# Attention C's scores on halves and strips of the TensorE array, and three loads and waits in another order

## The chip, the cores and the metric

One core of one Trainium2 chip runs the whole program in one launch. The metric is device microseconds (us) of that core, from the first to the last instruction with what the launch adds. TensorE (PE) multiplies, VectorE (DVE), ScalarE (ACT) and GpSimd (POOL) do the rest, and DMAs are issued from the queues of SyncE (SP) and ScalarE.

## The reference

A sequence of 1024 tokens of width 1024 passes a first block (four recurrent branches, a feed-forward part) and two attention layers. Two places matter here.

```python
# first block, feed-forward part (D_FF = 2816)
gate_up = xn @ w_ffn_in
g_ff, u_ff = jnp.split(gate_up, [D_FF], axis=-1)
h = h + (jax.nn.silu(g_ff) * u_ff) @ w_ffn_out
# second attention layer, attention C: 8 heads of 64 + 32 dimensions
q  = (rmsnorm(cq, g_cq) @ w_cq_b).reshape(B, S, 8, 96)
kv = (rmsnorm(ckv, g_ckv) @ w_ckv_b).reshape(B, S, 8, 64 + 64)
qc = rmsnorm(q, gq_c)                                      # then its last 32 rotated
kc = rmsnorm(concat([k_nope, k_pe of all heads], -1), gk_c) # then its last 32 rotated
oc = attend_blocks(qc, kc, v_c, 96 ** -0.5)                # softmax(q k^T) v
```

## The kernel before

Activations lie transposed: a tile `A(i)` (all of them in `AR`) or `R(i)` (in `ARR`) holds 128 features by 1024 tokens. PSUM is four tiles `ps` of 128 by 1024. TensorE's results go round these four: the n-th job (`opn`) takes tile n modulo 4 and first waits until the job four before it has been read (`freed`). So the order in which jobs are opened decides who waits for whom. Weights come in tiles `WR` (four of them), loaded by SyncE's queue in the order of the list `loads`, each when the job four weights earlier is done. Where fp32 is split into a high and a low part, GpSimd does it in the order of the list `splits`: a cast `WH<-WR` and a subtraction `WL<-WR,WH` (in the pairs also `ARR<-AR`).

**Feed-forward part.** Hidden tiles 0, 1 and 21 are plain products. The other 38 products go in 19 pairs by block products: seven half-size products (`product`, twelve matmuls each) in place of eight. They need sums of the weights (`weight_sums`, four VectorE subtractions or additions on 128x512) and sums of the input (`t_sum`, sixteen of 128x512 into `A(0..7)`), which ScalarE rounds to a high part (`R(16+j)`) and VectorE turns into a low part (`R(j)`, eight subtractions on 128x1024, semaphore `s_tlow`). The pairs' weights alternate between `A(8..11)` (even pairs) and `WR` (odd pairs); in the even case `A(8)` and `A(9)` receive the raw weights, so the first two of the four rounds of `t_sum` must have read them. GpSimd splits a pair's weights in four slots (`s_pair_split`), the first three of 128x1024, the last of 128x512. Then `ffn_out` multiplies the hidden tiles in three groups of 8, 8 and 6. A group's tiles are read back from HBM (`hidden` in `loads`), rounded by ScalarE (`hid_hi`) and subtracted by VectorE (`hid_lo`).

**Attention C.** `attend_pairs` makes 32 steps, eight blocks of 128 queries for each of four pairs of heads. In step s TensorE makes the scores `S` of both heads of block s (line 1273 of before), the output `O` of block s-2 (line 1284), and the transposes `T` of the probabilities of block s-1 (line 1295); `weave` then appends a piece of side work. On VectorE a step takes the maximum of each head's scores (line 3306), and ScalarE makes the exponentials (line 2375), whose end frees the score's PSUM tile, and then copies the transposes out (line 2385). Jobs per step are S0, S1, O, T0, T1. So T1 waits for the first exponential, and whatever TensorE opens behind T1 waits for the second:

```python
mm = pe.matmul(pt[:, h * 512:h * 512 + 512], q(p, m)[0:96, rows],
               k(p, m)[0:96, h * 512:h * 512 + 512], start=True, stop=True)
```

Attention B has the same steps, with head dimension 64: head 0 on rows 0 to 63 of the array and head 1 on rows 64 to 127, in turns. Beside C's steps the next heads are prepared, `prep_c(h)` in four steps a head, h from 2 to 7, and `prep_d(0)` in eight. For a head, TensorE makes query and key (lines 348), VectorE rotates the query's last 32 rows with three 32x1024 operations (`rotate`), and ScalarE scales and squares the key's own 64 rows and copies and squares the 32 rows that all heads share. Heads 4 and 6 also have a gate product (48 matmuls) in the step of the key. `prep_c0` prepares heads 0 and 1 ahead of the steps.

## Time and profile before

| | us |
|---|---|
| median of 3 runs | 3873.71 (3873.5 to 3878.88) |
| the profiled execution | 3871.55 |
| its span, first to last instruction | 3869.5 |
| mean granted TensorE clock | 0.984 |

The profile gives for each engine its busy time and its idle time with what ended it. A timeline row merges equal instructions in a row; a matmul on fp32 operands shows as two records, so the four score matmuls of a step are eight records.

### The profile page before, as it was taken

The page shows a single profiled execution, that of the slowest core. Times are in us where ns is not written, and L with a number is a line of the kernel's source. Part 1 is how long each engine was busy: PE and PEld are TensorE (multiplying, and loading weights), DVE is VectorE, ACT ScalarE, POOL GpSimd, SP SyncE. Part 2 cuts the span into 40 slices and gives each one's busy share as a digit, 9 for nine tenths or more (in the row PEclk, how much of TensorE's full clock was granted, in tenths as well). Part 3 has the DMA queues.
Part 4 walks back from the last instruction along what each step waited for, and adds up shares of the span by engine and source line. Part 5 has one row for each costly group of instructions (what it writes and reads, how often), then busy time and mean ns, then how long its engine had stood idle before and what let it go on. Part 6 is the DMA issues. An engine that isn't in the chain of part 4 may idle for free.

```text
span 3869.5 us, 51841 instructions
## 1 busy us (share of the span) xinstructions
PE 3706.4 (96%) x21561; PEld 2909.6 (75%) x21561; DVE 1985.1 (51%) x2505; ACT 1325.9 (34%) x1603; POOL 1018.0 (26%) x634
## 2 busy tenths in 40 slices
PE   8999999999999999999899999999999999999988
PEld 6778888878788887888788777666677566667767
DVE  8464455524652526333412556665754655456673
ACT  3243333322330112111201344455623666444450
POOL 4212222222233335666433411110022001111011
PEclk9999999999999999999999999999999999999999
DMA  4111111111125422222522211100121001111011
GB/s 146 34 50 50 44 53 47 50 44 47 55 79 182 147 88 66 86 83 82 195 78 70 85 43 43 44 17 9 53 66 54 14 13 27 31 25 25 17 55 68
DMA packets 283160, 238.56 MB, mean 62 GB/s; under 512 B 16976, under 2 KB 255728, under 8 KB 282928
## 3 DMA queue, kind: packets, MB, share of 16 engines
q1 hardware_dynamic: 262128, 166.04, 14.6%
q10 hardware_dynamic: 20800, 69.22, 5.0%
q8 instruction: 172, 2.82, 0.3%
q14 instruction: 60, 0.49, 0.0%
HBM read 181.81 MB, written 49.35 MB: 60 GB/s over the span
## 4 chain that ended last, share of the span: by engine, by line
PE 82%; DVE 11%; ACT 4%; issue 3%; POOL 1%; ACTq 0%; DMA 0%; DVEq 0%; SPq 0%; POOLq 0%
PE ps L401 19%; PE ps L418 18%; PE ps L451 15%; PE ps L902 9%; DVE AR L2474 3%; PE ps L1273 2%; DVE AR L2482 2%; DVE SM L3306 2%; PE ps L701 2%; PE ps L1284 1%; PE ps L1264 1%; PE ps L1295 1%; PE ps L503 1%; PE ps L1344 1%; PE ps L348 1%
## 5 line engine op out<-in xcount | busy, mean ns | idle before, releaser
L3439 POOL CAST WH<-WR 128x1024 fp32r<-128x1024 f32 (+2 forms) x231 | 240.8, 1043 | 2587.4 <-DMA WR<-in_w_in 827.1
L3441 POOL TENSOR_TENSOR WL<-WR,WH 128x1024 fp32r<-128x1024 f32 (+2 forms) x231 | 502.8, 2177 | 18.5
L2474 DVE TENSOR_TENSOR AR<-AR 128x512 f32<-128x512 f32 (+3 forms) x426 | 454.1, 1066 | 56.5 <-ACT AR L1822 38.1
L418 PE MATMUL ps<-ARR,WH 128*128 128x512 f32 x1472 | 367.1, 391 | 12.9 <-issue 10.7
L418 PEld LDWEIGHTS ps<-ARR,WH 128*128 128x128 f32 x1472 | 277.4, 189 | 71.6 <-issue 11.1
L401 PE MATMUL ps<-XH,WH 128*128 128x512 f32 (+2 forms) x1168 | 299.2, 399 | 4.6 <-POOL WL L3441 2.2
L401 PE MATMUL ps<-XH,WL 128*128 128x512 f32 (+2 forms) x1168 | 289.8, 390 | 0.0
L401 PE MATMUL ps<-XL,WH 128*128 128x512 f32 (+2 forms) x1168 | 288.6, 389 | 0.0
L401 PEld LDWEIGHTS ps<-XH,WH 128*128 128x128 f32 (+2 forms) x1168 | 215.9, 188 | 57.8 <-issue 8.0
L3306 DVE TENSOR_REDUCE SM<-ps 128x1 f32<-128x1024 f32 x128 | 156.8, 1225 | 197.3 <-PE ps L1273 116.1
L401 PEld LDWEIGHTS ps<-XH,WL 128*128 128x128 f32 (+2 forms) x1168 | 218.0, 187 | 48.8
L2474 DVE TENSOR_TENSOR H<-H,ps 128x1024 f32<-128x1024 f32 (+1 forms) x68 | 78.8, 1159 | 341.0 <-PE ps L418 340.7
L401 PEld LDWEIGHTS ps<-XL,WH 128*128 128x128 f32 (+2 forms) x1168 | 217.0, 186 | 48.0
L451 PE MATMUL ps<-XH,WH 128*128 128x512 f32 x864 | 236.5, 418 | 3.7 <-ACT AR L2315 2.3
L2482 DVE SCALAR_TENSOR_TENSOR AR<-ps,AR 128x512 f32<-128x512 f32 (+2 forms) x122 | 59.3, 486 | 341.5 <-ACT AR L1574 227.7
L2474 DVE TENSOR_TENSOR AR<-ps,AR 128x128 f32<-128x128 f32 (+2 forms) x193 | 102.1, 529 | 254.2 <-PE ps L902 220.7
L451 PE MATMUL ps<-XH,WL 128*128 128x512 f32 x864 | 214.4, 390 | 0.0
L451 PE MATMUL ps<-XL,WH 128*128 128x512 f32 x864 | 213.4, 389 | 0.0
L451 PEld LDWEIGHTS ps<-XH,WH 128*128 128x128 f32 x864 | 161.1, 197 | 57.3 <-issue 19.9
L451 PEld LDWEIGHTS ps<-XH,WL 128*128 128x128 f32 x864 | 163.1, 189 | 35.1
L451 PEld LDWEIGHTS ps<-XL,WH 128*128 128x128 f32 x864 | 162.2, 188 | 33.7
L2375 ACT ACTIVATE AR<-ps,SM,AR 128x1024 f32<-128x1024 f32 x112 | 135.0, 1205 | 152.2 <-DVE SM L2482 145.9
(295 smaller groups left out, 6257.3 us busy)
## 6 DMA issues: line engine op xcount, KB each, us to landing
WR<-in_w_in SPq DMA_DIRECT2D x78, 512.0 KB, 3.8
gates<-AR ACTq DMA_DIRECT2D x54, 512.0 KB, 2.8
AR<-gates SPq DMA_DIRECT2D x54, 512.0 KB, 4.3
H<-spill ACTq DMA_DIRECT2D x32, 512.0 KB, 5.9
WR<-in_w_in_e SPq DMA_DIRECT2D x26, 512.0 KB, 3.8
spill<-H ACTq DMA_DIRECT2D x24, 512.0 KB, 2.7
WR<-in_w_ffn_in SPq DMA_DIRECT2D x24, 512.0 KB, 3.8
WR<-in_w_in_o SPq DMA_DIRECT2D x23, 512.0 KB, 3.9
```

What stands on the lines that cost most here:

```text
L401: mm = pe.matmul(pt[0:m, h * 512:h * 512 + 512], wp[:, slot, k, 0:m], xp[:, k, h * 512:h * 512 + 512], start=i == 0, stop=i == 3 * KD - 1)
L418: mm = pe.matmul(pt[:, h * 512:h * 512 + 512], wp[:, w % 4, k, :], xp(k)[:, h * 512:h * 512 + 512], start=i == 0, stop=i == 3 * nk - 1)
L451: mm = pe.matmul(pt[:, h * 512:h * 512 + 512], wp[:, w % 4, k, :], xp[:, k, h * 512:h * 512 + 512], start=i == 0, stop=i == 3 * KD - 1)
L701: mm = pe.matmul(out, x1[r, c], later, start=True, stop=True)
L902: mm = pe.matmul(out, wp(i, slot)[:, 4 * half + k, :], xp(k), start=first and n == 0, stop=n == 11, skip_group_check=True)
L1273: mm = pe.matmul(pt[:, h * 512:h * 512 + 512], q(p, m)[0:96, rows], k(p, m)[0:96, h * 512:h * 512 + 512], start=True, stop=True)
L2375: act.activation(PROB[kind][i], PS[bank(("S", b, m))][:, :], ACT.Exp, scale=row_scale(kind, s, m), bias=SM[:, 20 + i:21 + i], accum_out=SM ...
L2474: return v.tensor_tensor(o, x, y, op)
L2482: return v.scalar_tensor_tensor(out=o, in0=x, scalar=s, in1=y, op0=op0, op1=op1)
L3306: v.tensor_reduce(SM[:, 34 + m:35 + m], PS[bank(("S", b, m))][:, :], AX.X, ALU.max)\
L3439: pool.tensor_copy(hi, full).then_inc(s_whi, 1)
L3441: pool.tensor_tensor(lo, full, hi, ALU.subtract).then_inc(s_wsplit, 1)
```

## The change

**Scores.** Each head's 96 rows are contracted in two parts. First 64 rows: head 0 on rows 0 to 63 of the array, head 1 on rows 64 to 127, as in attention B. Then the other 32 rows, as a strip of 32: the four matmuls (two heads, two halves of the keys) stand on four different strips. For that the even head has its 32 rotated rows twice, at rows 64 and 96, and the odd head has its own 64 at rows 64 to 127 and the rotated rows at 0 and 32. So the odd head's weights load in three parts, `rotate` has a fourth operation (`again`), and ScalarE copies the shared key rows twice.

**Block products.** VectorE makes the first pair's `weight_sums(0)` ahead of the eight low parts, and those in the order 0 to 7; TensorE's second product waits for four low parts, the third for eight; SyncE loads the first pair's weights after eight input sums.

**`ffn_out`.** The first two weights stand ahead of the hidden tiles' loads in SyncE's queue.

```diff
@@ block products and the list of loads (TensorE) @@
-                    pe.wait_ge(s_tlow, KD)
+                    pe.wait_ge(s_tlow, 4)
                 product(xz[:, 512:L], i, 1, 0, t_hi(0), t_lo(0)).then_inc(s_products, 1)
                 pe.wait_ge(freed[ny % 4], ny // 4)
+                if i == 0:
+                    pe.wait_ge(s_tlow, KD)
                 product(wy[:, 0:512], i, 1, 1, t_hi(3), t_lo(3)).then_inc(s_products, 1)
...
-            loads.append(("hidden", 0))
-            loads.append(("hidden", 1))
...
-                    if g == 1 and f == 4:
-                        loads.append(("hidden", 2))
+                    if (g, f) in ((0, 1), (0, 3), (1, 4)):
+                        loads.append(("hidden", {1: 0, 3: 1, 4: 2}[f]))
@@ prep_c, prep_c0 (TensorE) @@
+            def query_c(h):
+                if h % 2:
+                    gemm(("qc", h), (cols(wcq, h * 96 + 64, 32, nk=2), cols(wcq, h * 96, 64, nk=2)),
+                         rhs=lambda k: A(18 + k), nk=2)
+                else:
+                    gemm(("qc", h), cols(wcq, h * 96, 96, nk=2), rhs=lambda k: A(18 + k), m=96, nk=2)
+            def key_c(h):
+                gemm(("kc", h), cols(wckv, h * 128, 64, nk=1), rhs=lambda k: A(28), m=64, nk=1, at=h % 2 * 64)
@@ attend_pairs, kind "C" (TensorE) @@
-                            for m in range(2):
-                                pt, n = opn(("S", b, m))
+                            two = [opn(("S", b, m)) for m in range(2)]
+                            for pt, n in two:
                                 pe.wait_ge(freed[n % 4], n // 4)
...
+                            for h in range(2):
+                                for m, (pt, n) in enumerate(two):
+                                    e = slice(m * 64, m * 64 + 64)
+                                    pe.matmul(pt[:, h * 512:h * 512 + 512], q(p, m)[e, rows],
+                                              k(p, m)[e, h * 512:h * 512 + 512], start=True, stop=False,
+                                              skip_group_check=True)
+                            for h in range(2):
+                                for m, (pt, n) in enumerate(two):
+                                    e = slice(64 - m * 64 + h * 32, 96 - m * 64 + h * 32)
+                                    mm = pe.matmul(pt[:, h * 512:h * 512 + 512], q(p, m)[e, rows],
+                                                   k(p, m)[e, h * 512:h * 512 + 512], start=False, stop=True,
+                                                   skip_group_check=True)
+                                    if h:
+                                        mm.then_inc(filled[n % 4], 1)
@@ load (SyncE) @@
+                if isinstance(src, tuple) and m == P:
+                    for c in (0, 32):
+                        sp.dma_start(dst[:, 0:nk, c:c + 32], src[0]).then_inc(s_half_in, 16)
+                    sp.wait_ge(s_half_in, 16 * (dups[0] + 2))
+                    dups[0] += 2
+                    src, dst = src[1], dst[:, 0:nk, 64:P]
...
-                            sp.wait_ge(s_tsum, 16)
+                            sp.wait_ge(s_tsum, 8)
@@ prep_c (ScalarE), c = shared_at(h) @@
-                act.activation(kt[64:96, :], A(9)[96:128, :], ACT.Copy).then_inc(s_act_step, 1)
-                act.wait_ge(s_act_step, tick(s_act_step))
-                act.activation(A(22)[64:96, :], A(8)[96:128, :], ACT.Square).then_inc(s_kraw, 1)
+                for g in (c, c + 32):
+                    act.activation(kt[g:g + 32, :], A(26)[96:128, :], ACT.Copy).then_inc(s_act_step, 1)
+                    act.wait_ge(s_act_step, tick(s_act_step))
+                act.activation(A(22)[c:c + 32, :], A(25)[96:128, :], ACT.Square).then_inc(s_kraw, 1)
@@ block products, rotate (VectorE) @@
-            for n, j in enumerate((0, 4, 1, 5, 2, 6, 3, 7)):
-                v.wait_ge(s_thigh, n + 1)
+            weight_sums(0)
+            for j in range(KD):
+                v.wait_ge(s_thigh, 2 * (j % 4) + 1 + j // 4)
                 TT(R(j), A(j), R(16 + j), ALU.subtract).then_inc(s_tlow, 1)
                 v.wait_ge(s_tlow, tick(s_tlow))
-            weight_sums(0)
...
+                if again is not None:
+                    TT(x[again, :], x[rows, :], tmp[rows, :], ALU.add).then_inc(s_dve_step, 1)
+                    v.wait_ge(s_dve_step, tick(s_dve_step))
                 TT(x[rows, :], x[rows, :], tmp[rows, :], ALU.add).then_inc(s_rope_tmp, 1)
```

The instructions of the engines stand in another order at three places. SyncE's queue between the feed-forward part's last pair and `ffn_out`, before (`gates` holds the hidden tiles):

```order
117 L1511 DMA AR<-in_w_ffn_in 128x8x128
118 L1455 DMA WR<-in_w_ffn_in 128x8x128 x2
119 L1523 DMA AR<-gates 128x1024 x16
120 L1455 DMA WR<-in_w_ffn_out 128x8x128 x13
121 L1523 DMA AR<-gates 128x1024 x6
122 L1455 DMA WR<-in_w_ffn_out 128x8x128 x3
```

The same place of the changed program:

```order
117 L1538 DMA AR<-in_w_ffn_in 128x8x128
118 L1482 DMA WR<-in_w_ffn_in 128x8x128 x2
119 L1482 DMA WR<-in_w_ffn_out 128x8x128 x2
120 L1550 DMA AR<-gates 128x1024 x8
121 L1482 DMA WR<-in_w_ffn_out 128x8x128 x2
122 L1550 DMA AR<-gates 128x1024 x8
123 L1482 DMA WR<-in_w_ffn_out 128x8x128 x9
124 L1550 DMA AR<-gates 128x1024 x6
125 L1482 DMA WR<-in_w_ffn_out 128x8x128 x3
```

Two `ffn_out` weights now stand ahead of the first eight hidden tiles, and two more ahead of the next eight.

VectorE at the start of the block products, before, from the fifth of the eight low parts on (`ARR0`, `ARR1` are the low parts, `AR<-AR 128x512 x4` the weight sums of the first pair):

```order
468 L2474 TENSOR_TENSOR ARR0_51<-AR,ARR4_55 128x1024
469 L2474 TENSOR_TENSOR ARR1_52<-AR,ARR5_56 128x1024
470 L2474 TENSOR_TENSOR ARR0_51<-AR,ARR4_55 128x1024
471 L2474 TENSOR_TENSOR ARR1_52<-AR,ARR5_56 128x1024
472 L2474 TENSOR_TENSOR AR<-AR 128x512 x4
473 L2474 TENSOR_TENSOR AR<-AR,ps3 128x1024
474 L2474 TENSOR_TENSOR WR<-WR 128x512 x4
```

The changed program, from the input sums on:

```order
462 L2519 TENSOR_TENSOR AR<-AR 128x512 x16
463 L2519 TENSOR_TENSOR AR<-AR,ps1 128x1024
464 L2519 TENSOR_TENSOR AR<-AR 128x512 x4
465 L2519 TENSOR_TENSOR ARR0_51<-AR,ARR4_55 128x1024 x4
466 L2519 TENSOR_TENSOR ARR1_52<-AR,ARR5_56 128x1024 x4
467 L2519 TENSOR_TENSOR AR<-AR,ps3 128x1024
468 L2519 TENSOR_TENSOR WR<-WR 128x512 x4
```

The weight sums moved from behind the eight low parts to ahead of them.

TensorE in a step of attention C with a query's product behind it (line 348, in the changed program 349), before (scores on line 1273, in the changed program halves on 1286 and strips on 1292):

```order
2350 L1273 MATMUL ps<-AR 128x512 x4
2351 L1284 MATMUL ps<-AR 64x128 x16
2352 L1295 MATMUL ps<-CST,AR 128x128 x8
2353 L1295 MATMUL ps<-CST,MSK 128x128 x8
2354 L348 MATMUL ps<-AR,WR 96x512 x4
```

The same step of the changed program:

```order
2359 L1286 MATMUL ps<-AR 128x512 x4
2360 L1292 MATMUL ps<-AR 128x512 x4
2361 L1305 MATMUL ps<-AR 64x128 x16
2362 L1316 MATMUL ps<-CST,AR 128x128 x8
2363 L1316 MATMUL ps<-CST,MSK 128x128 x8
2364 L349 MATMUL ps<-AR,WR 96x512 x4
```

Four score matmuls became four on halves and four on strips; what follows them is the same.

## Rows read from the trace of the kernel before

**Rows 1.** The page's busy time of each engine: busy us, share of the span, instructions.
```profile
PE 3706.4 (96%) x21561; PEld 2909.6 (75%) x21561; DVE 1985.1 (51%) x2505; ACT 1325.9 (34%) x1603; POOL 1018.0 (26%) x634
```

**Rows 2.** Timeline, SyncE's DMA queue alone: start us, us, engine line, out<-in, count.
```profile
1856.67 0.99 SPq L1455 DMA_DIRECT2D WR<-in_w_ffn_in  x2
```

**Rows 3.** Timeline 1868 to 1912, start of `ffn_out`; in brackets: idle before, releaser.
```profile
1875.71 12.09 SPq L1523 DMA_DIRECT2D AR<-gates  x16
...
1887.85 22.12 SPq L1455 DMA_DIRECT2D WR<-in_w_ffn_out  x4
...
1891.58 1.06 ACT L1940 ACTIVATE ARR<-AR 128x1024 fp32r<-128x1024 f32 x1 [0.21 <-DMA AR<-gates]
...
1904.85 3.20 POOL L3441 TENSOR_TENSOR WL<-WR,WH 128x1024 fp32r<-128x1024 f32 x1
...
1908.15 3.72 PE L418 MATMUL ps<-ARR,WH 128*128 128x512 f32 x8 [10.71 <-issue]
```

**Rows 4.** Timeline, the next matmuls of `ffn_out`.
```profile
1911.70 2.02 PE L418 MATMUL ps<-ARR,WL 128*128 128x512 f32 x8
```

**Rows 5.** Busy us (instructions) of PE, PEld, DVE, ACT, POOL; PEclk, DMA share, GB/s.
```profile
1902.00:1911.00 9.00, 2.85 (x7) 2.30 (x8) 6.47 (x4) 7.51 (x8) 4.24 (x2) 0.50 1.07 382
```

**Rows 6.** Timeline 1462 to 1496, VectorE beside GpSimd, then the first pair's weights.
```profile
1469.61 10.53 DVE L2474 TENSOR_TENSOR XL<-AR,XH 128x1024 fp32r<-128x1024 f32 x4
...
1471.83 1.92 POOL L3439 CAST WH<-WR 128x1024 fp32r<-128x1024 f32 x1
...
1477.14 1.92 POOL L3439 CAST WH<-WR 128x1024 fp32r<-128x1024 f32 x1
...
1488.12 2.16 ACT L1947 ACTIVATE ARR<-AR 128x1024 fp32r<-128x1024 f32 x2 [0.71 <-DVE AR L2474]
...
1493.87 0.37 SPq L1508 DMA_DIRECT2D AR<-in_w_ffn_in  x1
```

**Rows 7.** Timeline 1490 to 1545, the first block products.
```profile
1495.13 10.04 DVE L2474 TENSOR_TENSOR ARR<-AR,ARR 128x1024 fp32r<-128x1024 f32 x8
...
1505.21 2.87 DVE L2474 TENSOR_TENSOR AR<-AR 128x512 f32<-128x512 f32 x4
...
1511.72 3.78 PE L902 MATMUL ps<-XH,ARR 128*128 128x512 f32 x8 [6.71 <-POOL ARR L3451]
...
1530.08 2.88 PE L902 MATMUL ps<-ARR,ARR 128*128 128x512 f32 x12
...
1532.80 1.07 PE L902 MATMUL ps<-XH,WH 128*128 128x512 f32 x4
```

**Rows 8.** Timeline 2593 to 2607, one step of attention B with nothing beside it.
```profile
2593.15 1.99 PE L1264 MATMUL ps<-AR 64*128 64x512 f32 x8 [0.30 <-ACT AR L2375]
...
2595.24 1.23 DVE L3306 TENSOR_REDUCE SM<-ps 128x1 f32<-128x1024 f32 x1 [1.09 <-PE ps L1264]
...
2596.69 1.23 DVE L3306 TENSOR_REDUCE SM<-ps 128x1 f32<-128x1024 f32 x1
...
2599.58 1.99 PE L1264 MATMUL ps<-AR 64*128 64x512 f32 x8 [0.30 <-ACT AR L2375]
```

**Rows 9.** Timeline 3111 to 3167, two steps of attention C.
```profile
3111.31 3.60 PE L1273 MATMUL ps<-AR 96*128 96x512 f32 x8
...
3115.01 1.22 DVE L3306 TENSOR_REDUCE SM<-ps 128x1 f32<-128x1024 f32 x1 [0.30 <-PE ps L1273]
...
3118.54 1.84 PE L984 MATMUL ps<-CST,AR 96*128 96x2 f32 x16
...
3138.38 1.05 ACT L2231 ACTIVATE AR<-AR 32x1024 f32<-32x1024 f32 x1
...
3139.47 1.21 ACT L2375 ACTIVATE AR<-ps,SM,AR 128x1024 f32<-128x1024 f32 x1
```

**Rows 10.** Timeline 3082 to 3120, VectorE rotates a query of attention C.
```profile
3081.24 3.72 DVE L2474 TENSOR_TENSOR AR<-AR 32x1024 f32<-32x1024 f32 x3
```

**Rows 11.** Chain of work that ended last, before attention C: start us, us, what.
```profile
3002.39 1.23 DVE AR L2474
```

More of the change, by code:

```diff
@@ L54 @@
 CE = CEPS2 + 1
-CW = {n: CE + 8 + i * 70 for i, n in enumerate(["w64", "w96", "w128", "w256", "w1024", "weps"])}
+CW = {n: CE + 8 + i * 70 for i, n in enumerate(["w64", "w96", "w128", "w256", "w1024", "weps", "w96_odd"])}
 NCST = CE + 8 + len(CW) * 70
@@ L347, in gemm @@
                     for k in range(nk):
-                        mm = pe.matmul(pt[0:m, h * 512:h * 512 + 512], WR[0:kp, w % 4, k, 0:m],
+                        mm = pe.matmul(pt[at:at + m, h * 512:h * 512 + 512], WR[0:kp, w % 4, k, 0:m],
                                        rhs(k)[0:kp, h * 512:h * 512 + 512], start=k == 0, stop=k == nk - 1)
@@ L1268, in attend_pairs @@
                         else:
-                            for m in range(2):
-                                pt, n = opn(("S", b, m))
+                            two = [opn(("S", b, m)) for m in range(2)]
+                            for pt, n in two:
                                 pe.wait_ge(freed[n % 4], n // 4)
-                                for h in range(2):
-                                    mm = pe.matmul(pt[:, h * 512:h * 512 + 512], q(p, m)[0:96, rows],
-                                                   k(p, m)[0:96, h * 512:h * 512 + 512], start=True, stop=True)
-                                mm.then_inc(filled[n % 4], 1)
+                            for h in range(2):
[12 more added lines that the diff above has]
+                                        mm.then_inc(filled[n % 4], 1)
                     if s >= 2:
@@ L2092, in tables @@
             def tables(which):
-                act.dma_start(A(25), a["rope"][2 * which]).then_inc(s_tab_in, 16)
-                act.dma_start(A(26), a["rope"][2 * which + 1]).then_inc(s_tab_in, 16)
+                rows = slice(0, 96 if which == 1 else P)
+                act.dma_start(A(25)[rows, :], a["rope"][2 * which][rows, :]).then_inc(s_tab_in, 16)
+                act.dma_start(A(26)[rows, :], a["rope"][2 * which + 1][rows, :]).then_inc(s_tab_in, 16)
             def gate(name, dst):
@@ L2194, in shared_key, with shared_at, own_rows, own_gain @@
             def shared_key(h, square):
-                act.activation(A(CK[h % 4])[64:96, :], A(9)[96:128, :], ACT.Copy).then_inc(s_act_step, 1)
-                act.wait_ge(s_act_step, tick(s_act_step))
-                act.activation(square[64:96, :], A(8)[96:128, :], ACT.Square).then_inc(s_act_step, 1)
-                act.wait_ge(s_act_step, tick(s_act_step))
+                for r in (0, 32):
+                    act.activation(A(CK[h % 4])[shared_at(h) + r:shared_at(h) + r + 32, :], A(26)[96:128, :], ACT.Copy)\
+                        .then_inc(s_act_step, 1)
+                    act.wait_ge(s_act_step, tick(s_act_step))
+                act.activation(square[shared_at(h):shared_at(h) + 32, :], A(25)[96:128, :], ACT.Square)\
+                    .then_inc(s_act_step, 1)
+                act.wait_ge(s_act_step, tick(s_act_step))
+            def shared_at(h):
+                return 0 if h % 2 else 64
+            def own_rows(h):
+                return slice(h % 2 * 64, h % 2 * 64 + 64)
+            def own_gain(h):
+                c = PC["gkc_odd" if h % 2 else "gkc"]
+                return PAR[own_rows(h), c:c + 1]
             def own_key(h, square):
                 act.wait_ge(filled[bank(("kc", h))], turn(("kc", h)))
-                t = PS[bank(("kc", h))]
-                act.activation(A(CK[h % 4])[0:64, :], t[0:64, :], ACT.Copy, scale=par("gkc", 0, 64)).then_inc(s_act_step, 1)
+                t, r = PS[bank(("kc", h))], own_rows(h)
+                act.activation(A(CK[h % 4])[r, :], t[r, :], ACT.Copy, scale=own_gain(h)).then_inc(s_act_step, 1)
                 act.wait_ge(s_act_step, tick(s_act_step))
-                act.activation(square[0:64, :], t[0:64, :], ACT.Square)\
+                act.activation(square[r, :], t[r, :], ACT.Square)\
                     .then_inc(freed[bank(("kc", h))], 1)
@@ L2213, in prep_c @@
                 act.wait_ge(s_rope_tmp, 6 + h)
-                raw(("qc", h), A(CQ[h % 4]), A(22), 96, par("gqc", 0, 96), (A(27), (64,), 16, s_rot_in[0]))
+                if h % 2:
+                    raw(("qc", h), A(CQ[h % 4]), A(22), P, par("gqc_odd"), (A(27), (0,), 16, s_rot_in[0]))
+                else:
+                    raw(("qc", h), A(CQ[h % 4]), A(22), 96, par("gqc", 0, 96), (A(27), (64,), 16, s_rot_in[0]))
                 yield
@@ L3068, in _, with rotate @@
             turns = [0, 0]
-            def rotate(x, tmp, ndma, rows=slice(0, P), i=0):
+            def rotate(x, tmp, ndma, rows=slice(0, P), i=0, again=None):
                 turns[i] += 16 * ndma
@@ L3120, in prep_c0 @@
                 for h in range(2):
[L3121 removed]
+                    kb(A(CK[h]), P, ("hb", cnt["hn"] - 2 + h))
                 yield
@@ L3126, in prep_c @@
                 hq(RS[h % 4], 96 ** -0.5)
-                rotate(A(CQ[h % 4]), A(27), 2, slice(64, 96))
+                rotate(A(CQ[h % 4]), A(27), 2, *((slice(0, 32), 0, slice(32, 64)) if h % 2 else (slice(64, 96), 0, slice(96, P))))
                 yield
@@ L3130, in prep_c @@
                 yield
-                kb(A(CK[h % 4]), 96)
+                kb(A(CK[h % 4]))
                 yield
@@ L3481, in constants @@
         cst[:min(n, P), CW[f"w{n}"] + 6:CW[f"w{n}"] + 8] = 1.0 / n
+    for r in (slice(0, 32), slice(64, P)):
+        cst[r, CW["w96_odd"] + 6:CW["w96_odd"] + 8] = 1.0 / 96
     cst[:, CW["weps"] + 6:CW["weps"] + 8] = EPS / 1024
@@ L3520, in constants @@
     table(0, "pB", [(b + o, 16, ang) for b in (0, 64) for o, ang in ((0, row), (32, col))])
-    table(1, "pC", [(64, 16, angles(t, 32, 10000.0))])
+    table(1, "pC", [(b, 16, angles(t, 32, 10000.0)) for b in (0, 64)])
     part = angles(t, 16, 500000.0)
@@ L3563, in pack @@
     put("gkc", g("gk_c_2")[0])
+    for k, n in (("gqc_odd", "gq_c_2"), ("gkc_odd", "gk_c_2")):
+        put(k, np.concatenate([g(n)[0][64:], g(n)[0][64:], g(n)[0][:64]]))
     put("gsub", g("g_sub_d_2")[0])
```

42 lines of the change are left out of this document (21 added, 21 removed).

## The prediction

> **What bounds the kernel now.** I read the page first: TensorE is busy for 96% of the span [rows 1], so what counts is its idle time and its own work. Then the chain of waits, for its longest single waits, and the timeline at those places. Two are in the feed-forward part: 10.71 us ahead of `ffn_out` [rows 3] and 6.71 us ahead of the first block product [rows 7]. Then the timeline of attention C, step by step, to see what ends each wait there; a step counts here from its first score matmul to the first side job behind T1. Fifteen of C's 32 steps have a light one: the score matmuls start at 3111.31, VectorE's second maximum at 3115.01 (3.70 later), and TensorE reaches the job behind T1 at 3118.54, after 7.23 [rows 9]; fourteen of them take 7.15 to 7.31, the fifteenth is the last step, below. Nothing waits in them: they are TensorE's own work. Attention B shows the same step with scores on halves. There the first maximum starts 2.09 after the scores (2593.15 to 2595.24), and the next scores start 4.34 after that maximum, held by the second exponential, not by TensorE [rows 8].
>
> **The `ffn_out` weights.** Before, SyncE issued sixteen hidden tiles from 1875.71 to 1887.80 and only then the weight, whose low part GpSimd ended at 1904.85 + 3.20 = 1908.05; TensorE started at 1908.15, 10.71 late [rows 3]. Changed, two weights stand right behind the last `ffn_in` weights, issued from 1856.67 [rows 2], some 31 us earlier. What is late next are the hidden tiles: group 0's last high part ended at 1891.58 + 1.06 = 1892.64 [rows 3], 4.8 us before TensorE's place at 1908.15 - 10.71 = 1897.44. So the wait goes whole. The wait also cost clock: in 1902 to 1911 the granted clock was 0.50 [rows 5], that is 1.2 and not 2.4 GHz, and the first eight matmuls took 1911.70 - 1908.15 = 3.55 [rows 3, 4] where twelve take 1532.80 - 1530.08 = 2.72 [rows 7], so eight 1.81: 1.74 more. Term: -(10.71 + 1.74) = **-12.4**. The second group's tiles move back behind two more weights; they are wanted eight jobs later, and cost nothing. If that cover were gone, at most the old 10.7 would come back.
>
> **The first block products.** Wanted is a start at 1511.72 - 6.71 = 1505.01. Half the input sums are done at 1488.12, so the weights can be issued 1493.87 - 1488.12 = 5.75 earlier [rows 6], and are there when VectorE gets to the weight sums at 1495.13 (its place for the low parts before). These take 2.87, to 1498.0; before they ran from 1505.21 [rows 7]. GpSimd's first slot is then in time for 1505. But now GpSimd splits while VectorE makes the eight low parts, of the same kind (128x1024 to fp32r, two SBUF inputs) as four that ran beside GpSimd's splits a little earlier: those took 10.53, that is 2.63 each, and GpSimd needed 1477.14 - 1471.83 = 5.31 for a slot [rows 6]; alone, eight low parts took 10.04, 1.26 each [rows 7]. So the second slot and the fourth low part are both ready at about 1498.0 + 10.6 = 1508.6, when the first product (2.72) has ended at 1507.7: 0.9 lost. The third product wants all eight. GpSimd's three full slots take 15.9 and cover six low parts; for the last two beside the short slot I estimate half a slot and one op alone, 2.65 + 1.26 = 3.9: 1498.0 + 15.9 + 3.9 = 1517.8. TensorE stands again from 1511.3, 6.5 us, and pays the clock again: before, the seven products took 1532.80 - 1511.72 = 21.08 where 7 x 2.72 = 19.04 are due, 2.04 more. End of the first pair: 1517.8 + 5 x 2.72 + 2.04 = 1533.4, against 1532.80 [rows 7]: **+0.6**. If the two engines do not hinder each other, all is in time and -(6.71 + 2.04) = -8.8 results; that is the lower bound. Upper: both fully one after the other, 8 x 2.63 = 21 to 1519, +1.8.
>
> **The scores.** From B to C the second set of four rounds on the array puts the maximum from 2.09 to 3.70 after the start [rows 8, 9]. Changed, there are four matmul slots on halves (as B's) and one round in which four strips run together, half as long as B's whole: six units for B's four and C's eight, so (2.09 + 3.70) / 2 = 2.90. No row shows four strips at once, nor a change from halves to strips. Upper bound: strips run only two at a time, eight units, 3.70. I take 3.05, close to the lower, since two halves ran fully together in B. TensorE saves 0.65 us a step by that, some 21 us over 32 steps, and that is not what the kernel gets: both heads' scores now end together, so the first maximum starts at 3.05 and no longer while the second head's scores are still made, and the job behind T1 comes 4.34 after it [rows 8], at 7.39. Against 7.23 [rows 9] a light step is 0.16 *longer*: fourteen make +2.2 (bounds 7.24, +0.1; 8.04, +11). In the last step TensorE waits for copies behind the second exponential; the second maximum moves from 3.70 to 3.05 + 1.45 (2596.69 - 2595.24 [rows 8]) = 4.50: +0.8. In the five steps with the key's norm in front, the first maximum stands behind VectorE's work on that norm, before and after: nothing. The first two steps, the one behind the first key and the three of `prep_d(0)` with longer chains I take at nothing, between -1 and +1 together.
>
> The Trainium skill ("TensorE: Matmul & The Clock Gate", Part 3) gives four row strips a measured 3.07 times the speed of one after another, not four times; by it the strip round would be 0.26 longer if 0.80 is its length at four times. The skill ("TensorEngine Tiling (Array Packing)", Key Properties) also says that changing the tiling mode drains TensorE, which speaks against two modes in a step. By both, a light step comes to about 7.5, and the fourteen to +4 instead of +2.2.
>
> **The preparation of heads.** Of six heads, four (2, 3, 5, 7) have the rotation on VectorE directly ahead of the step's first maximum: three operations in 3.72 [rows 10], 1.24 each. The fourth adds **1.24** to the step. For heads 4 and 6 the gate product covers the rotation, but ScalarE's work on the key runs to the exponential: copies and squares end 3138.38 + 1.05 = 3139.43, the first exponential starts at 3139.47 [rows 9]. One more copy adds **1.05**. Scores ending earlier help neither. Sum 4 x 1.24 + 2 x 1.05 = +7.1. In `prep_c0` both rotations are on the chain that ended last, six pieces of 1.23 from 3002.39 on [rows 11]; two more make +2.5. ScalarE's extra copies there lie beside the second gate product. The odd queries' weights load in three parts with a wait between; they are issued about a head, four steps, ahead, and even the load behind sixteen others took only 1887.85 to about 1903.7 [rows 3]. Uncovered, it would cost a landing, some 5 us, in four heads.
>
> **Sum** against the profiled execution's 3871.55 us (span 3869.5 and 2.05 around it; the median, 3873.71, is 2.2 above): -12.4 + 0.6 + 2.2 + 0.8 + 7.1 + 2.5 = +0.8. Some clock will be lost at the longer waits of the key's steps, for one of which I add 0.5 on average: 3872.9, and on the scale of the median **3875.0**. A difference under 0.2%, 7.7 us, can't be told from none.
>
> **Rivals.**
> - *No hindrance at the block products.* VectorE and GpSimd overlap freely: -8.8 in place of +0.6, 3866. Against it stand rows 6. Chance 0.10, half of it on the faster side.
> - *The key's steps have slack.* If the added operations find room there (the steps' waits are inferred from releasers), +7.1 falls away: 3868. Chance 0.08.
> - *The scores gain what TensorE saves.* 0.65 x 32 = -21 in place of +2.2 and +0.8: 3851. It needs the exponentials earlier than 4.34 behind the first maximum, and B, in the same code, shows they aren't. Chance 0.05.
> - *Strips run two at a time* (or the change of mode costs as much): maximum at 3.70, light steps 8.04; fourteen of them and the five behind the norm 0.81 each, the last 3.70 + 1.45 - 3.70 = 1.45: 16.8 in place of 3.0, 3889, slower. It decides from 3.4 on. Chance 0.12.
> - *The clock falls in the key's steps.* They wait at T1 for the exponential already, and now 1.05 to 1.24 longer. If each of six loses what `ffn_out`'s start lost (1.74), +10.4: 3885, slower; four of six are enough. Chance 0.15.
> - The forecast, 3869 to 3881: 0.50.
>
> **Numbers.** Range 3865 to 3887: it leaves out the scores' full gain, most of the two-at-a-time case, and little else. Faster by over 0.2% (under 3866): 0.05, half of 0.10, and 0.03 of the second rival: 0.13. Slower (over 3881.4): 0.12 + 0.15 and 0.01: 0.28. Within: 0.59.
>
> **What the changed profile would show.** TensorE goes into `ffn_out` with no wait over 1 us and no half clock. At the block products the first starts near 1505, and one wait of 5 to 7 us stands ahead of the third, ended by VectorE; low parts of 2 to 3 us beside GpSimd. In C the halves and strips end about 3.0 after their start, the first maximum 3.05, the job behind T1 7.4, its wait ended by the exponential (line 2375 before); key steps 1.05 to 1.24 longer. I am wrong if light steps get shorter than 7.1, or if the low parts take 1.26 each beside the splits.

## The result and the profile after

The changed kernel takes 3895.28 us (median of 5 runs, 3893.64 to 3903.11), the kernel before 3873.71 beside it: 1.0055 of it, 95% interval 1.0041 to 1.0069. It is slower by 21.6 us, where I had said 1.3, and outside my range. The profiled execution took 3894.96, its span 3893.0, with a mean granted clock of 0.982.

**Into `ffn_out`** the wait is gone. The timeline there; the first row is GpSimd's subtraction for the second `ffn_out` weight, its last one before a gap of 18 us:

```profile
1872.94 2.41 POOL L3489 TENSOR_TENSOR WL<-WR,WH 128x1024 fp32r<-128x1024 f32 x1
...
1897.36 1.98 PE L419 MATMUL ps<-ARR,WH 128*128 128x512 f32 x8
```

Both weights are split at 1872.94 + 2.41 = 1875.35, and TensorE starts at 1897.36 straight behind its own work (no idle time stands in the row). Before it was 1908.15 [rows 3].

**The first block products**, again the timeline:

```profile
1497.74 18.64 DVE L2519 TENSOR_TENSOR ARR<-AR,ARR 128x1024 fp32r<-128x1024 f32 x8
...
1504.56 1.98 PE L903 MATMUL ps<-XH,ARR 128*128 128x512 f32 x8
...
1508.54 3.01 PE L903 MATMUL ps<-ARR,ARR 128*128 128x512 f32 x12 [1.10 <-POOL ARR L3499]
...
1516.52 8.37 PE L903 MATMUL ps<-ARR,ARR 128*128 128x512 f32 x24 [4.97 <-DVE ARR L2519]
...
1532.88 1.07 PE L903 MATMUL ps<-XH,WH 128*128 128x512 f32 x4
```

Eight low parts take 18.64, 2.33 each; the first product starts at 1504.56, TensorE waits 1.10 ahead of the second and 4.97 ahead of the third, and the pair ends at 1532.88, where it ended at 1532.80 [rows 7]. That is the picture forecast, place by place.

**Attention C** is where the time went. From its first score matmul to attention D's first transposes, 408.3 us before (3017.19 to 3425.52) became 444.4 (3005.45 to 3449.86): +36.1, where I had some 10 in these steps. A light step (nothing in front of the maxima but the scores) without a split of a weight, step 16, steps counted from 0:

```profile
3192.04 1.99 PE L1286 MATMUL ps<-AR 64*128 64x512 f32 x8 [1.53 <-issue]
...
3193.96 1.14 PE L1292 MATMUL ps<-AR 32*128 32x512 f32 x8
...
3195.03 1.97 PE L1305 MATMUL ps<-AR 128*64 128x128 f32 x32
3195.22 1.22 DVE L3354 TENSOR_REDUCE SM<-ps 128x1 f32<-128x1024 f32 x1 [3.38 <-PE ps L1292]
3196.48 0.16 DVE L2527 SCALAR_TENSOR_TENSOR SM<-SM,AR 128x1 f32<-128x1 f32 x1
...
3197.93 0.16 DVE L2527 SCALAR_TENSOR_TENSOR SM<-SM,AR 128x1 f32<-128x1 f32 x1
...
3198.20 1.06 PE L1316 MATMUL ps<-CST,MSK 128*128 128x128 f32 x8 [0.17 <-ACT AR L2420]
3198.21 1.21 ACT L2420 ACTIVATE AR<-ps,SM,AR 128x1024 f32<-128x1024 f32 x1 [0.16 <-DVE SM L2527]
...
3199.56 3.67 PE L349 MATMUL ps<-AR,WR 128*96 128x512 f32 x8 [0.30 <-ACT AR L2420]
```

Halves from 3192.04, strips from 3193.96, the scores' end at 3195.03, after 2.99. The first maximum starts 3.18 after the scores, the job behind T1 (3199.56) 4.34 after that, 7.52 in all: the forecast had 3.05, 4.34 and 7.39. TensorE now waits in such a step, 0.17 and 0.30, where it did not wait at all. A step in which GpSimd splits a weight (step 12) looks otherwise:

```profile
3146.53 1.99 PE L1286 MATMUL ps<-AR 64*128 64x512 f32 x8
...
3149.71 1.23 DVE L3354 TENSOR_REDUCE SM<-ps 128x1 f32<-128x1024 f32 x1 [3.69 <-PE ps L1292]
3150.65 1.04 POOL L3487 CAST WH<-WR 128x1024 fp32r<-128x1024 f32 x1 [98.89 <-DMA WR<-in_w_in_o]
3150.97 0.73 DVE L2527 SCALAR_TENSOR_TENSOR SM<-SM,AR 128x1 f32<-128x1 f32 x1
...
3151.76 2.36 POOL L3489 TENSOR_TENSOR WL<-WR,WH 128x1024 fp32r<-128x1024 f32 x1
...
3152.99 1.15 DVE L2527 SCALAR_TENSOR_TENSOR SM<-SM,AR 128x1 f32<-128x1 f32 x1
...
3154.25 1.20 ACT L2420 ACTIVATE AR<-ps,SM,AR 128x1024 f32<-128x1024 f32 x1 [1.15 <-DVE SM L2527]
...
3155.69 1.06 PE L469 MATMUL ps<-CST,AR 128*128 128x128 f32 x8 [1.37 <-ACT AR L2420]
```

The small operation behind a maximum (128x1, two operands: it negates and scales it for the exponential) takes 0.73 in place of 0.16, and the second 1.15. Both end just behind GpSimd's instruction: 3150.97 + 0.73 = 3151.70 and GpSimd's cast 3150.65 + 1.04 = 3151.69; 3152.99 + 1.15 = 3154.14 and the subtraction 3151.76 + 2.36 = 3154.12. The second exponential starts at 3154.25, 7.72 after the scores, and the job behind T1 at 9.16, not 7.52. The same step of the kernel before:

```profile
3153.60 3.60 PE L1273 MATMUL ps<-AR 96*128 96x512 f32 x8
...
3156.85 0.16 DVE L2482 SCALAR_TENSOR_TENSOR SM<-SM,AR 128x1 f32<-128x1 f32 x1
...
3157.77 1.04 POOL L3439 CAST WH<-WR 128x1024 fp32r<-128x1024 f32 x1 [90.99 <-DMA WR<-in_w_in_o]
...
3158.56 0.26 DVE L2482 SCALAR_TENSOR_TENSOR SM<-SM,AR 128x1 f32<-128x1 f32 x1
3158.89 2.37 POOL L3441 TENSOR_TENSOR WL<-WR,WH 128x1024 fp32r<-128x1024 f32 x1
3158.94 1.21 ACT L2375 ACTIVATE AR<-ps,SM,AR 128x1024 f32<-128x1024 f32 x1 [0.52 <-DVE SM L2482]
...
3159.72 2.08 DVE L2478 TENSOR_SCALAR AR<-AR,SM 128x1024 f32<-128x1024 f32 x1
```

GpSimd's split began 4.17 after the scores' start, where it is 4.12 now, but the small operations stood at 3.25 and 4.96: one ahead of it, the other at the end of the cast (0.26, to 3158.82; the cast ends at 3158.81). The large operation at 3159.72 did wait, 2.08, and nobody waited for it.

**A step with the key's norm in front** (step 15) has a wait on VectorE that I had ruled out. Ahead of its first maximum VectorE now stands idle 0.48 for the last strips, where before the maximum followed VectorE's own work on the norm without such a wait (at 2.76 after the scores' start; now 3.18):

```profile
3184.92 1.23 DVE L3354 TENSOR_REDUCE SM<-ps 128x1 f32<-128x1024 f32 x1 [0.48 <-PE ps L1292]
```

T1's waits for the exponential in C (TensorE, 3000 to 3450: line waited at, total, times, longest), and C's window, whose granted clock (third number from the end) is 0.95 of full speed:

```profile
PE ps L1316 <- ACT AR L2420: 19.5, 30, 2.9
```

```profile
3005.00:3450.00 445.00, 396.28 (x2870) 259.68 (x2871) 238.98 (x393) 230.76 (x293) 33.90 (x20) 0.95 0.08 19
```

Before, T1's line had 5.8 us of such waits in 5 places, and in C the clock was 0.99. By the trace's record of the clock, 41.0 us of C now ran at half clock, and 10.7 before:

```profile
PE ps L1295 <- ACT AR L2375: 5.8, 5, 1.4
```

```profile
3017.00:3425.00 408.00, 390.34 (x2610) 264.40 (x2611) 226.02 (x386) 224.43 (x287) 34.01 (x20) 0.99 0.09 21
```

### The profile page after: what moved, and what is told of

It is laid out like the page before. It is cut to its first block, busy times and chain, and to the rows that moved or that the text cites. A ratio compares the mean times of both kernels' runs of the same rounds, so it can differ in the third digit from the quotient of the medians.

```text
span 3893.0 us, 52410 instructions
## 1 busy us (share of the span) xinstructions
PE 3707.5 (95%) x21817; PEld 2903.6 (75%) x21817; DVE 1998.5 (51%) x2513; ACT 1334.5 (34%) x1611; POOL 1021.3 (26%) x634
## 3 DMA queue, kind: packets, MB, share of 16 engines
q8 instruction: 174, 2.85, 0.3%
## 4 chain that ended last, share of the span: by engine, by line
PE 79%; DVE 13%; ACT 4%; issue 3%; POOL 0%; DMA 0%; ACTq 0%; SPq 0%; DVEq 0%; POOLq 0%
PE ps L402 19%; PE ps L419 17%; PE ps L452 15%; PE ps L903 9%; DVE SM L3354 3%; DVE AR L2519 3%; PE ps L702 2%; DVE AR L2527 2%; PE ps L1286 1%; PE ps L1275 1%; PE ps L504 1%; PE ps L1365 1%; PE ps L349 1%; DVE SM L2527 1%; PE ps L1375 1%
```

## The experiments

Theories after the result. **A:** the maxima end later, and in ten of C's steps that carries the two small operations into GpSimd's split. **B:** behind the new waits, short in nearly every step and longer in the key's steps, TensorE's granted clock falls to half, and its work then takes longer. **C:** the preparation itself, or the strips, cost more than forecast. Ten kernels ran.

**1. Attention C as before** (the rows of C's change all undone).

> The changed kernel with all of attention C's change undone: the order of the block products and the ffn_out weights stay. The trace of the changed kernel has attention B's start 14.3 us earlier than before, and all of the loss in C. If that is so, this kernel takes 3873.7 - 14.3 = 3859.4 us, C's steps take the 393.2 us that they took before, and C's change alone costs about 36 us. My forecast had 3873.7 - 12.4 + 0.6 = 3861.9 and only 13 us for C. If the loss in C came from what lies ahead of it (another phase of the clock), C would be longer here too, and the time over 3865.

Measured: 3857.77 us, 0.9957 [0.9945, 0.997] of before. C took 402.5, 5.8 less than before with the same instructions, and the windows show why:

```profile
3009.00:3412.00 403.00, 385.52 (x2613) 262.70 (x2614) 225.88 (x387) 224.42 (x287) 34.02 (x20) 1.00 0.08 21
```

The clock there is 1.00 in place of 0.99. So one execution of the same steps differs from another by some us of clock. Five kernels here have C's scores and preparation as before: in the traces of before and of 1, 5, 6 and 10, C took 408.3, 402.5, 405.9, 407.8 and 408.9, with 10.7, 0, 6.8, 10.4 and 13.7 us of it at half clock. Each is near 402.5 plus half of its time at half clock. C's change alone costs 37.5 us, the difference of the medians.

**2. Whole scores on the new layout.** The odd heads' 32 rotated rows count twice in it, so it computes other numbers, and so does kernel 9.

```diff
-                            two = [opn(("S", b, m)) for m in range(2)]
...
+                            for m in range(2):
+                                pt, n = opn(("S", b, m))
+                                pe.wait_ge(freed[n % 4], n // 4)
+                                for h in range(2):
+                                    mm = pe.matmul(pt[:, h * 512:h * 512 + 512], q(p, m)[0:96 + 32 * m, rows],
+                                                   k(p, m)[0:96 + 32 * m, h * 512:h * 512 + 512], start=True, stop=True)
+                                mm.then_inc(filled[n % 4], 1)
```

> The changed kernel, its layout of queries and keys and its preparation of heads kept, but each head's scores made by whole matmuls again, one head after the other (rows 0 to 95 for the even head; all 128 rows for the odd head, which counts its 32 rotated rows twice, so the scores of odd heads are other numbers). Theory: the loss lies in when the maxima end, since in ten steps GpSimd's split of a weight then holds VectorE's two small operations behind them. Here the first maximum starts at 1.99 and the second at 3.70 again, the small operations take 0.2 to 0.3, light steps are 7.2 again and only the preparation's added operations are left: C's loop 393 + 7 = 400 to 404, total 3895.3 - 27 = 3868 (3865 to 3872). Rival, the preparation is what costs (copies, rotation, the clock that falls in its waits): the time stays above 3880.

Measured: 3877.20, 1.001 [0.9999, 1.0021]. The light steps and those with a split are at 7.2 again, so A holds for them; but the kernel stays 19.4 above the first one. Its step 10 (gate product and key), behind ScalarE's added copy:

```profile
3125.68 1.05 ACT L2266 ACTIVATE AR<-AR 32x1024 f32<-32x1024 f32 x1
3126.77 1.20 ACT L2410 ACTIVATE AR<-ps,SM,AR 128x1024 f32<-128x1024 f32 x1
...
3128.20 1.94 PE L1306 MATMUL ps<-CST,MSK 128*128 128x128 f32 x8 [2.21 <-ACT AR L2410]
...
3130.07 1.75 PE L481 MATMUL ps<-AR,CST 96*64 96x128 f32 x16
```

```profile
3001.00:3425.00 424.00, 399.86 (x2610) 270.67 (x2611) 233.51 (x392) 230.83 (x293) 34.76 (x20) 0.96 0.08 20
```

T1 waits 2.21, and then its eight transposes take 1.94 where they take 1.06 to 1.09 at full clock, and the next sixteen matmuls 1.75 for 1.09. The added copy is 1.05, but the step grew by 12.38 - 10.10 = 2.28.

**3. The splits held** until the step's second small operation.

```diff
+                    t = used.get(w - 4)
+                    if t is not None and t < 31 and (used[w] is None or used[w] > t + 1):
...
+                        pool.wait_ge(s_negmax, before_c[0] + 2 * t + 4)
                     pool.tensor_copy(hi, full).then_inc(s_whi, 1)
```

(`used[w]` is the step in which weight w is used.)

> The changed kernel, and GpSimd's ten splits of weights in C's steps wait until the second small operation of that step (the negated, scaled maximum, 128x1) is done; the weights are wanted three to eight steps later. Theory: the small operations take 0.16 again in place of 0.72 and 1.14, both exponentials come 0.56 and 1.54 earlier, and the ten steps shorten by 1.54 to 2.0 each, with less clock lost: 3895.3 - 15 to - 22, about 3876. Rival: GpSimd then hinders VectorE's next operations (the scaling of the probabilities, 0.75 each, which T waits for a step later) and nothing is won: 3893 to 3895. Rival, the clock is the cause and not the wait: less than 5 us won.

Measured: 3885.82, 1.0024 [1.0014, 1.0035]: 9.5 less. Step 12:

```profile
3157.42 0.16 DVE L2532 SCALAR_TENSOR_TENSOR SM<-SM,AR 128x1 f32<-128x1 f32 x1
...
3157.74 1.04 POOL L3497 CAST WH<-WR 128x1024 fp32r<-128x1024 f32 x1 [100.90 <-DVE SM L2532]
```

The small operation takes 0.16, and in the five light steps with a split the job behind T1 comes at 7.61 in place of 9.10 to 9.25. Step 18 wins nothing, since ScalarE's work on the key runs to 7.39 anyway; steps 22, 25 and 26 win 1.26, 0.69 and 1.24, the last step about 1.5. That makes 12 and not 15 to 22, and the median gave 9.5; C's clock stayed at 0.95. The rival's hindrance is there too, one of the two scalings of the probabilities in step 12 takes 2.54 in place of 0.75, but TensorE doesn't wait for it.

**4. One operand in the small operation,** in attention B and C.

```diff
-                            STT(SM[:, 20 + i:21 + i], SM[:, 34 + m:35 + m], -1.0, row_scale(kind, s, m), ALU.mult, ALU.mult)\
+                            TS(SM[:, 20 + i:21 + i], SM[:, 34 + m:35 + m], row_scale(kind, s, m), -1.0, ALU.mult, ALU.mult)\
```

> The changed kernel, with VectorE's small operation behind each maximum in attention B and C written with one tensor operand (tensor_scalar with the scale as a per-partition scalar and -1 as the second) in place of two. If it is the second tensor operand in SBUF that makes it wait for GpSimd, the operation takes 0.16 beside GpSimd's work too, and the time falls as with the splits held, to about 3878. If every VectorE operation on SBUF alone waits, nothing changes: 3893 to 3897. The second is likelier: the scaling of the probabilities has one tensor operand, and it took 2.08 beside a split in the kernel before, 0.75 alone.

Measured: 3886.28, 1.0032 [1.0019, 1.0045], 9.0 less. The likelier guess was wrong: the one-operand form does not wait. Step 20, in the middle of a subtraction:

```profile
3264.95 2.37 POOL L3489 TENSOR_TENSOR WL<-WR,WH 128x1024 fp32r<-128x1024 f32 x1
...
3265.90 0.21 DVE L2524 TENSOR_SCALAR SM<-SM,AR 128x1 f32<-128x1 f32 x1
...
3266.68 1.19 DVE L2523 TENSOR_SCALAR AR<-AR,SM 128x1024 f32<-128x1024 f32 x1
```

It takes 0.21 or 0.22 in all ten steps, 0.05 more than the other form alone. The scaling of the probabilities has one operand too, but of 128x1024, and it still waits: it ends at 3266.68 + 1.19 = 3267.87, 0.55 behind the subtraction (3267.32), and takes 2.21 in step 12. So the number of operands alone does not decide it; whether it is the size isn't tested.

**5. `ffn_out`'s loads alone.**

> The kernel before with nothing but the changed order of the ffn_out loads. My forecast had 10.71 of wait and 1.74 of clock, -12.4; in the changed kernel attention B's start lay 14.3 earlier than before. So 3874.4 - 12.4 to - 14.3 = 3860 to 3862. If part of the gain is the block products' (whose end moved by 0.1 in the trace), or only another phase of the clock, it is less than 10.

Measured: 3857.53, 0.9961 [0.995, 0.9972]: -15.1, between -19.4 and -10.8. The 12.4 lie in the interval.

**6. The block products alone.**

> The kernel before with nothing but the changed order around the first block products. Forecast: VectorE and GpSimd hinder each other, low parts of 2.3 to 2.6 us, a wait of 5 us ahead of the third product, +0.6; in the changed kernel's trace the first pair ended 0.1 later than before. So 3874 to 3876. The rival (they overlap freely) would have 3866.

Measured: 3875.01, 1.0002 [0.9989, 1.0015]: +0.8, between -4.3 and +5.8. TensorE waits 1.14 and 4.92 there, as in the changed kernel.

**7. TensorE's waits in C filled**, on kernel 4. `beside` is the PSUM tile of O, of which only the first 128 columns are read.

```diff
+                            if kind == "C" and m and s >= 2:
+                                thrown(beside, {2: 14, 6: 2, 10: 12, 14: 8, 18: 12, 25: 5, 26: 2, 27: 8}.get(s, 1))
                             pe.wait_ge(freed[n % 4], n // 4)
...
+                        if kind == "C" and s >= 2:
+                            thrown(beside, 2)
```

> The kernel with the one-operand operation (3886.3), and TensorE fills its waits in C's steps with matmuls of 128 columns whose result nobody reads (one ahead of T1, two behind it, more in the steps where T1 waits over 1 us). That kernel has 42.5 us of waits over 50 ns in C and 47.6 us at half the clock there; the one with C as before has 18.5 and none. Theory: the short waits in nearly every step bring the half clock, which costs up to half of its time, 15 to 20 us; with the waits filled nearly all of it goes: 3886 - 12 to - 18 = 3868 to 3874, and C under 6.8 us at half clock. Rival: the clock falls for another reason, and the matmuls change nothing or lengthen the steps: 3886 to 3892.

Measured: 3882.11, 1.0027 [1.0016, 1.0037], 4.2 less. C took 427.2 in place of 436.5, and its clock rose from 0.95 (kernel 4, first) to 0.98:

```profile
3008.00:3445.00 437.00, 395.32 (x2867) 257.53 (x2868) 230.66 (x393) 230.77 (x293) 33.97 (x20) 0.95 0.08 20
```

```profile
3015.00:3442.00 427.00, 413.59 (x3162) 287.18 (x3163) 233.08 (x393) 230.96 (x293) 34.77 (x20) 0.98 0.08 20
```

C's steps gave 9.3 us in this execution, less than the 12 to 18 expected, but the two profiled executions as wholes took the same, 3889.20 and 3889.28, and the medians differ by only 4.2 (3880.28 to 3889.20 and 3876.68 to 3889.28), which isn't clear of noise. In C's trace the clock rose as theory B has it; that the kernel gains by it isn't shown here.

**8. Strips two at a time**, on kernel 4; without the fourth operation of `rotate`.

```diff
-                                    e = slice(64 - m * 64 + h * 32, 96 - m * 64 + h * 32)
+                                    e = slice(64 - m * 64, 96 - m * 64)
...
-                for g in (c, c + 32):
+                for g in ((c, c + 32) if h < 4 else (c,)):
```

> The kernel with the one-operand operation (3886.3), with each head's strips both on the same 32 rows, so that only two strips can run at once; so the fourth operation of rotate is left out, and ScalarE's second copy for heads 4 to 7. The computation is the whole one. Theory: the strips take 2 x 0.8 in place of 1.07, the first maximum comes at 3.8 in place of 3.18 and a light step is 0.6 longer, 13 in 22 such steps; the preparation gives back 1.24 in four steps, 1.05 in two and 2.5 in prep_c0, 9.6, and some clock: 3884 to 3890. Rival (four strips were never four at once): the first maximum stays near 3.2 and the time falls to about 3876.

Measured: 3901.52, 1.0074 [1.0058, 1.0091]. Step 7:

```profile
3086.98 1.99 PE L1286 MATMUL ps<-AR 64*128 64x512 f32 x8
...
3088.90 1.99 PE L1292 MATMUL ps<-AR 32*128 32x512 f32 x8
...
3090.81 1.97 PE L1305 MATMUL ps<-AR 128*64 128x128 f32 x32
3090.98 1.23 DVE L3351 TENSOR_REDUCE SM<-ps 128x1 f32<-128x1024 f32 x1 [1.30 <-PE ps L1292]
```

The strips take 3090.81 - 3088.90 = 1.91 in place of 1.07, so four strips do run together; the first maximum comes at 4.00 and the job behind T1 at 8.54, both 0.82 later than in kernel 4. The step follows the first maximum one to one. The kernel is 15.2 slower, more than expected: each step costs 0.82 and not 0.6, and the first maximum is at 4.00 in 26 of 32 steps, those of the key's norm too, and not in 22. 26 x 0.82 less the 9.6 of the preparation is 11.7; what the other 3.5 are isn't shown, and is within the uncertainty of such a difference.

**9. Whole scores, and the waits at T1 filled** in eight steps: kernel 2 with `thrown(beside, {2: 11, 6: 5, 10: 9, 14: 5, 18: 9, 22: 10, 25: 3, 27: 4}[s])` ahead of T1's wait.

> The kernel with the whole scores on the new layout (3877.2; its odd heads' rotated rows count twice), and TensorE fills its waits at T1 in eight steps, those of the keys' norm and gates above all, with matmuls of 128 columns that nobody reads. The preparation's added operations should cost 7.1 + 2.5 = 9.6, but that kernel is 19.4 above the one with C as before. Theory: the rest is clock, lost behind the longer waits at T1 (34 us at half clock in C's steps, where C as before had none). With the waits filled C has under 10 us at half clock, and the time is 3857.8 + 9.6 = 3867, at most 3870. Rival: the preparation costs more by itself, and the time stays at 3875 to 3878.

Measured: 3865.57, 0.9979 [0.9966, 0.9991]: 11.6 less than without them, and 7.8 above kernel 1. Step 10 and C's clock:

```profile
3129.42 2.17 PE L1261 MATMUL ps<-CST 128*128 128x128 f32 x18
3130.36 1.21 ACT L2419 ACTIVATE AR<-ps,SM,AR 128x1024 f32<-128x1024 f32 x1
...
3131.71 1.09 PE L1315 MATMUL ps<-CST,MSK 128*128 128x128 f32 x8
...
3133.13 1.09 PE L481 MATMUL ps<-AR,CST 96*64 96x128 f32 x16 [0.33 <-ACT AR L2419]
```

```profile
3008.00:3420.00 412.00, 399.28 (x2721) 275.99 (x2722) 234.07 (x391) 231.23 (x293) 34.63 (x20) 1.00 0.09 21
```

Nine thrown matmuls (eighteen records) stand in the wait, T1 starts at the same point behind the exponential (1.35 after its start; in kernel 2, 1.43), and now runs at full clock. The step is 11.20 long: 1.10 more than kernel 1's 10.10, which is the added copy's 1.05 and hardly more. In C's steps 3.4 us are left at half clock, of 31.5 in kernel 2.

**10. C as before, with the one-operand form.**

> The kernel with C as before (3857.8) and the one-operand operation behind the maxima of B and C. Theory: with the maxima at 1.99 and 3.70 the small operations end before GpSimd's subtraction begins, so here the operand costs nothing: 3855 to 3861. Rival: the hindrance costs time in B or in C's other steps too, and 3 us or more are won.

Measured: 3858.53, 0.996 [0.9946, 0.9974], as kernel 1. Where the small operations fall outside GpSimd's split, or have room, the form changes nothing.

The steps side by side, from the timelines: first the start of the job behind T1, then the step's length, each after its first score matmul. Step 24 is light, 12 is light with a split, 14 has a rotation on VectorE directly in front of the first maximum, 10 has gate product and key.

| | step 24 | step 12 | step 14 | step 10 |
|---|---|---|---|---|
| before | 7.22, 18.22 | 7.23, 11.54 | 7.97, 9.00 | 9.07, 10.10 |
| 1, C as before | 7.22, 18.22 | 7.23, 11.53 | 7.97, 8.99 | 9.07, 10.10 |
| after | 7.51, 18.64 | 9.16, 13.59 | 8.73, 9.78 | 10.16, 12.06 |
| 2, whole scores | 7.22, 18.22 | 7.23, 11.54 | 9.21, 10.23 | 10.70, 12.38 |
| 3, splits held | 7.52, 18.62 | 7.61, 12.04 | 8.38, 9.44 | 10.19, 12.10 |
| 4, one operand | 7.62, 18.73 | 7.72, 12.14 | 9.32, 10.37 | 10.34, 12.25 |
| 9, whole, filled | 7.22, 18.22 | 7.23, 11.54 | 9.21, 10.24 | 10.17, 11.20 |

## Why the prediction was wrong

By the medians, from C as before (3857.8) to the changed kernel (3895.3): the preparation with its waits filled +7.8 (kernel 9), its waits unfilled +11.6 (kernel 2), the scores' halves and strips, with the clock that their waits cost, +9.1 (kernel 4), the two-operand form beside GpSimd +9.0. Each difference is uncertain by some 5 us, and they depend on the order: with the splits held in place of the form changed, the last two are +8.6 and +9.5. Against the forecast three terms were too small: the clock (0.5), by 11.1; the splits (nothing), by 9.0; the scores (2.2 + 0.8), by 6.1. The two other edits together came out 4.1 better than forecast, the preparation 1.8 better. The splits are an error of mechanism, and so is a part of the scores' 6.1, the key's norm; the clock had its mechanism among my rivals and was mis-sized in the sum.

- **`ffn_out`, -12.4.** Right: -15.1, interval -19.4 to -10.8.
- **Block products, +0.6.** Right: +0.8, and in each place: hindrance between VectorE and GpSimd, the third product's wait of 4.97 (6.5 forecast), the end of the pair +0.1. The rival without hindrance (3866) falls.
- **The light step, 7.39.** The mechanism was right: the first maximum sets the step, 4.34 later comes the job behind T1 (7.51 to 7.61 in the light steps without a split, once 7.74; kernel 8 moved both by 0.82). The first maximum is at 3.18, not 3.05. The strips take 1.07, where 2.90 - 2.09 = 0.81 would be four times the speed of one after another. The Trainium skill ("TensorE: Matmul & The Clock Gate", Part 3) has a measured 3.07 times for four row strips, which would make 0.80 x 4 / 3.07 = 1.04 of it, an estimate (the prediction's 0.26 should be 0.24), and the trace agrees. The Trainium skill ("TensorEngine Tiling (Array Packing)", Key Properties) has a drain at a change of mode; no row here shows it apart from the rest. Halves take 1.92 to the first strip, and strips two at a time directly behind halves 1.91 (kernel 8).
- **What a light step grew by.** I had reckoned only to the start of the job behind T1. In step 24 that start came 0.29 later, but the step grew by 0.42, since the job's own matmuls took 0.13 longer (18.64 - 7.51 against 18.22 - 7.22); they now start behind a wait of 0.30. Of the nine light steps without a split seven grew by 0.4 to 0.6, and steps 5 and 13 by 1.0, with 1.1 to 1.2 us at half clock in each. Without the clock's part the nine make some 4, where +2.2 was said for all fourteen.
- **The key's norm, "before and after: nothing".** Wrong. The norm's work ends ahead of the strips now, so the first maximum moves from 2.76 to 3.18, and the job behind T1 from 7.43 to 7.60 where the clock holds (steps 3, 7 and 15). It is some 0.2 a step.
- **The step that failed: "the job comes 4.34 after the first maximum" was taken for every light step, and what GpSimd does at that time was never looked at.** The figure comes from B, in a step without a split. Five of the fourteen light steps, the last one and four others have a split at some 4.1 to 7.6 after the scores' start. Moving the small operations from 3.25 and 4.96 to 4.44 and 6.46 puts both inside. I had used the same hindrance, from [rows 6], for the block products. What the runs showed in its place: the small operations take 0.7 and 1.1 in place of 0.16, and in the five light steps the job behind T1 comes at 9.10 to 9.25, some 6.0 after the first maximum in place of 4.34. Kernels 3 and 4, which remove this in two ways, win 9.5 and 9.0. The Trainium skill ("SBUF — State Buffer", Who interferes with whom) says that a VectorE operation with two SBUF inputs and a GpSimd instruction that reads SBUF block each other for a whole instruction, by who starts first, and that one with a single input does so only in its fast modes. The rows agree on two inputs: 0.73 and 1.15, to the end of GpSimd's instruction within 0.02. With one input it is 0.21 for the small form and 2.21 for the large; which of them ran in a fast mode no row says.
- **The preparation, +7.1 and +2.5.** Right within the measurement: kernel 9 has +7.8 for both, and in its trace 1.24 to 1.26 in steps 2, 6 and 14, 1.10 in steps 10 and 18, and 2.16 in step 22, in which a split adds its part. But that is with the clock held up. Where the step ahead loses clock, its longer time covers part of the rotation: with 0, 1.1 and 2.2 us at half clock in step 13 (kernel 4, the changed kernel, kernel 3) step 14's first maximum came at 4.78, 4.30 and 3.78. So the terms don't add up independently.
- **The clock, 0.5.** Mis-sized, and the largest miss: 11.6, kernel 2 against 9. My rival "the clock falls in the key's steps" had this mechanism and its price, 10.4, and I gave it 0.15. What spoke for it was in my own text: in the two steps with a gate product T1 waited 1.1 already, and an added 1.05 doubles it. In the traces of before and of kernels 1, 5, 6 and 10, where these two wait 1.12, neither has any time at half clock; in the changed kernel and in 2, 3 and 4, where they wait 2.2 to 2.85, both have, 1.0 to 3.4 us each time. In the changed kernel more clock is lost than this. If time at half clock costs half of itself, as in the five executions under experiment 1, its 41.0 us cost some 20 us, an estimate, and 15 of the 36.1 that C grew by. That the short waits in all steps bring the part beyond 11.6 is argued: kernel 7's gain isn't clear of noise.

The sum by measured terms: 3873.7 - 15.9 (kernel 1) + 7.8 + 11.6 + 9.1 + 9.0 = 3895.3, as it must be. Open is how the clock's loss divides between the single waits: a wait of 1.39 in step 2 was followed by 6 us at half clock in step 3 of the kernel before, and by none in kernel 1.

The version that beats both kernels is the first one, C as before with the other two edits: 3857.8. The `ffn_out` edit alone does as well (3857.5).

## What to carry to other kernels

A step that is bound by a chain through other engines gets longer when TensorE's work is made shorter in a way that starts the chain later: ask when the first link starts, not when the last matmul ends. When a piece of a chain moves in time, list everything that the other engines do in its new place, small operations included: here a 0.16 us operation behind GpSimd's instruction cost as much as the whole reordering. And price a longer TensorE wait with the clock behind it, above all when waits of a similar length come back in every few steps.

## What the runs showed of the hardware

- A 128x1 VectorE operation with two SBUF operands takes 0.16 alone and up to 2.35 beside GpSimd (step 18 of kernel 1), ending with GpSimd's instruction; the same with one operand and a per-partition scalar takes 0.21 or 0.22, also in the middle of GpSimd's subtraction, in all ten steps. The 128x1024 one-operand operation waits (2.21 for 0.75).
- Four strips of 32 rows, 512 columns of fp32: 1.07 together, 1.91 two at a time.
- Throw-away matmuls in the waits at T1 of eight steps brought C's granted clock from 0.96 to 1.00 and the kernel from 3877.2 to 3865.6 (kernels 2 and 9).
- Time of TensorE at half clock cost about half of itself: 402.5, 405.9, 407.8, 408.3 and 408.9 us for C with 0, 6.8, 10.4, 10.7 and 13.7 us at half clock.
